# Residual linears run by thirds of the tokens in one chain, and a cross attention that writes w_xo's split inputs itself

## What is computed

```python
for layer in range(DEPTH):
    h = rms_norm(x, norm_mix_g[layer])
    y = ab_mixer(h) if layer % 2 == 0 else c_mixer(h)     # each ends in @ w_out
    x = x + y
    x = x + mem_xattn(rms_norm(x, norm_xa_g[layer]), mem_k[layer], mem_v[layer], xa_wq[layer], xa_wo[layer])
return rms_norm(x, norm_final_g)

def mem_xattn(h, mk, mv, wq, wo):          # 4 heads of 256, 256 memory tokens
    q = (h @ wq).reshape(...)
    p = softmax(einsum(q, mk) * 256 ** -0.5)
    o = einsum(p, mv)
    return o @ wo
```

## Time and profile before

| | us |
|---|---|
| median of 3 runs | 3328.08 (3316.22 to 3329.48) |
| the profiled execution, its own time | 3325.3 |
| its span, first to last instruction | 3323.6 |
| PE busy | 2883.9 (87%) |
| DVE / ACT / POOL busy | 1528.6 / 862.4 / 596.9 |
| mean granted PE clock | 0.920 of full speed |

### The profile page before, as it was taken

One profiled execution on the slowest core, in us unless ns is written; L12 is line 12 of the kernel. 1 busy time (PEld: TensorE's weight loads), 2 busy tenths in 40 slices (PEclk: granted clock), 3 DMA queues, 4 the chain that ended last, 5 costly groups with the idle time before them and its releaser, 6 DMA issues. The chain is left out here.

```text
span 3323.6 us, 46167 instructions
## 1 busy us (share of the span) xinstructions
PE 2883.9 (87%) x17599; PEld 2553.3 (77%) x17599; DVE 1528.6 (46%) x1933; ACT 862.4 (26%) x1330; POOL 596.9 (18%) x536
## 2 busy tenths in 40 slices
PE   7989999678767888888888999999898899888887
PEld 7988888334437887887578999999777789888657
DVE  6267876875466763341434121111455542340423
ACT  5211112556751011221222000011222232220231
POOL 0002222656612321200010120000322302100011
PEclk9989999889978988898998999999987899989988
DMA  7379997875134102313631322222555352213641
GB/s 263 123 246 326 366 328 259 252 218 154 33 144 141 38 32 72 104 58 133 228 111 49 114 108 83 100 95 83 182 180 189 120 178 93 99 37 122 212 153 64
DMA packets 240146, 489.51 MB, mean 147 GB/s; under 512 B 37897, under 2 KB 98954, under 8 KB 239634
## 3 DMA queue, kind: packets, MB, share of 16 engines
q1 hardware_dynamic: 220690, 420.65, 37.3%
q0 software_dynamic: 15120, 51.46, 4.4%
q10 hardware_dynamic: 4176, 15.32, 1.1%
HBM read 378.83 MB, written 112.78 MB: 148 GB/s over the span
## 5 line engine op out<-in xcount | busy, mean ns | idle before, releaser
L414 PE MATMUL ps<-in_hi,w_hi 128*128 128x344 f32 x2496 | 806.7, 323 | 93.4 <-DVE in_lo L317 93.4
L415 PE MATMUL ps<-in_lo,w_hi 128*128 128x344 f32 x2496 | 804.1, 322 | 0.0
L416 PE MATMUL ps<-in_hi,w_lo 128*128 128x344 f32 x2496 | 803.1, 322 | 0.0
L414 PEld LDWEIGHTS ps<-in_hi,w_hi 128*128 128x128 f32 x2496 | 474.7, 190 | 97.2 <-DVE in_lo L317 97.2
L416 PEld LDWEIGHTS ps<-in_hi,w_lo 128*128 128x128 f32 x2496 | 475.0, 190 | 0.0
L415 PEld LDWEIGHTS ps<-in_lo,w_hi 128*128 128x128 f32 x2496 | 474.8, 190 | 0.0
L273 DVE CAST w_hi<-w_raw 128x1024 fp32r<-128x1024 f32 x64 | 46.9, 732 | 512.9 <-PE ps L416 499.7
L277 POOL TENSOR_TENSOR w_lo<-w_raw,w_hi 128x1024 fp32r<-128x1024 f32 x40 | 95.3, 2387 | 1029.3 <-ACT w_hi L273 1029.3
L1523 PE MATMUL ps<-in_hi,wv_hi 128*128 128x344 f32 x696 | 228.4, 328 | 2.1 <-DVE wv_lo L1371 2.1
L1525 PE MATMUL ps<-in_hi,wv_lo 128*128 128x344 f32 x696 | 223.4, 321 | 0.0
L1524 PE MATMUL ps<-in_lo,wv_hi 128*128 128x344 f32 x696 | 223.4, 321 | 0.0
(11 more groups left out here) (351 smaller groups left out, 5272.7 us busy)
## 6 DMA issues: line engine op xcount, KB each, us to landing
k_pages<-in_cache_k SPq DMA_DIRECT2D x256, 256.0 KB, 4.6
v_pages<-in_cache_v POOLq DMA_DIRECT2D x160, 256.0 KB, 5.4
cc<-stage SPq DMA_DIRECT2D x48, 516.0 KB, 2.7
v_pages<-in_cache_v SPq DMA_DIRECT2D x96, 256.0 KB, 3.0
w_raw<-in_w_c SPq DMA_DIRECT2D x48, 512.0 KB, 4.3
in_raw<-og SPq DMA_DIRECT2D x40, 516.0 KB, 5.5
kq_raw<-in_w_mem SPq DMA_DIRECT2D x32, 512.0 KB, 4.0
xs_kv<-in_mem_k SPq DMA_DIRECT2D x16, 1024.0 KB, 7.2
```

What stands on the lines that cost most here:

```text
L414: pe.matmul(o, w_hi[:, u, a:b], h, start=(kt == 0), stop=False)
L415: pe.matmul(o, w_hi[:, u, a:b], l, start=False, stop=False)
L416: return pe.matmul(o, w_lo[:, u, a:b], h, start=False, stop=(kt == KT - 1))
```

## The change

`final_norm` goes, and the linears with a residual no longer use `linear`. A new function `chain` runs one to three passes as one block, all of it by thirds of the tokens: product n is output tile n % 8 of third n // 8 % 3 of pass n // 24, 24 matmuls of 344 columns, in PSUM bank n % 6. All eight weight tiles of a pass are kept, split, in SBUF (one copy; each is replaced when its last third is done), with two raw buffers. Residual additions, squares, their sums (bank 6 or 7), the scaling and the split of a normed input are each 344 columns wide and stand in each engine's order at steps n written out by `sum_at`, `norm_at`, `weight_at` and `load_at`. There is no hardware loop. The chains are w_oab + w_xq; w_xo; w_oc first half + second half + w_xq; w_xo + final norm (its last scalings, two per step, are stored in pairs of tiles). w_c keeps `linear`.

`cross_attend` gets w_xo's input buffers `hi` and `lo`. ACT's `copy_out` writes `hi` rounded, DVE's new `out_low` writes the remainder from PSUM and raises `oc_done`; nothing is stored to or loaded from `og`. The first two raw tiles of w_xo are loaded at the end of SP's queue in the attention (`early`).

The diff, cut to its core:

```diff
+def chain(k, passes, hi, lo, final=None, early=None):
...
+    BANKS, SUM_BANK = 6, 6
+    RAW = 2
+    PASS = NCH * KT
+    N = PASS * len(passes)
+    READY = passes[0].load is None
+    R = sum(p.norm is None for p in passes)
+    RES = PASS * R
+    SQ0 = RES - PASS
+    RATE = 2 if final else 1
+    END = N + (KT if final else 3)
...
+        def sum_at(n):
+            c = (n - SQ0) // KT - 1
+            return c if NORMED and 0 <= c < NCH and (n - SQ0) % KT == (3 if n < N else 2) else None
+        def norm_at(n):
+            found = []
+            for c in range(NCH):
+                first = SQ0 + KT * (c + 1) + (4 if SQ0 + KT * (c + 1) < N else 3)
+                if NORMED and first <= n < first + KT // RATE:
+                    found += [(c, RATE * (n - first) + j) for j in range(RATE)]
+            return found
+        def weight_at(n):
+            found = [m for m in (n + 2,) if 2 <= m < KT]
+            for p in range(1, len(passes)):
+                t = n - 1 - (PASS * p - KT)
+                if 0 <= t < KT:
+                    found.append(KT * p + t)
+            return found
...
+        @block.sync
...
+            def weights(m):
+                if m >= RAW:
+                    sp.wait_ge(*low(m - RAW))
+                p = passes[m // KT]
+                sp.dma_start(raw[:, m % RAW, :], p.w[p.w0 + m % KT]).then_inc(loaded[m % RAW], 16)
...
+            for n in range(END):
+                at = load_at(n)
+                if at:
+                    inputs(*at)
+                for m in weight_at(n):
+                    weights(m)
+                if RES < n <= N:
+                    store(n - 1)
...
         @block.scalar
...
+            def high(m):
+                act.wait_ge(loaded[m % RAW], 16 * (m // RAW + 1))
+                if m >= KT:
+                    act.wait_ge(mm_done, PASS * (m // KT) - KT + m % KT + 1)
+                act.copy(w_hi[:, m % KT, :], raw[:, m % RAW, :]).then_inc(hi_done, 1)
...
+            for n in range(END):
+                if sum_at(n) is not None:
+                    inverse_root(sum_at(n))
+                if RES < n <= N:
+                    evacuate(n - 1)
+                at = load_at(n)
+                if at:
+                    input_high(*at)
+                for m in weight_at(n):
+                    high(m)
+                if SQ0 < n <= RES:
+                    square(n - 1)
+                if not final:
+                    for c, kt in norm_at(n):
+                        normed_high(c, kt)
+        @block.gpsimd
+        def _(pool):
+            for m in range(int(READY), KT * len(passes)):
+                split_low(pool, m).then_inc(lo_done, 1)
+        @block.vector
...
+            for n in range(END):
+                if 0 < n <= RES:
+                    resid(n - 1)
+                if SQ0 < n - 1 <= RES and (n - 2) % KT:
+                    add_squares(n - 2)
+                at = load_at(n)
+                if at:
+                    input_low(*at)
+                if not final:
+                    for c, kt in norm_at(n - 1):
+                        normed_low(c, kt)
+                for c, kt in norm_at(n):
+                    scaled(c, kt)
...
         @block.tensor
...
+            for n in range(2, END):
+                if sum_at(n) is not None:
+                    squares_sum(sum_at(n))
...
+                if n >= BANKS:
+                    pe.wait_ge(*((resid_done, n - BANKS + 1) if n - BANKS < RES else (out_done, n - BANKS - RES + 1)))
+                for kt in range(KT):
+                    product(n, kt)
...
-def cross_attend(k, xq, kv, kv0, mem_k, mem_v, s0, og):
+def cross_attend(k, xq, kv, kv0, mem_k, mem_v, s0, hi, lo, early):
...
+            raw, loaded, w, w0 = early
             for u in range(2):
-                sp.wait_ge(stored[u], 16 * (NBATCH // 2))
+                sp.dma_start(raw[:, u, :], w[w0 + u]).then_inc(loaded[u], 16)
...
+            def out_low(n):
+                dve.wait_ge(oh_done, n + 1)
+                dve.tensor_tensor(half_of(lo, n), ps[:, 4:6, :], half_of(hi, n).bitcast(f32), ALU.subtract).then_inc(oc_done, 1)
...
             for n in range(NBATCH):
+                if n >= 1:
+                    out_low(n - 1)
                 if n + 1 < NBATCH:
                     maxima(n + 1)
                 beside(n, 0)
...
             def copy_out(n):
                 act.wait_ge(o_done, n + 1)
-                if n >= 2:
-                    act.wait_ge(stored[n % 2], 16 * (n // 2))
-                act.copy(o[:, n % 2], ps[:, 4:6, :]).then_inc(oc_done, 1)
+                act.copy(half_of(hi, n), ps[:, 4:6, :]).then_inc(oh_done, 1)
...
-        project_out(ins["w_oab"], 0, 0)
+        project_out(Pass(ins["w_oab"], 0, load=(og, 0)), queries(0))
         cross_attention(0)
...
-        for half in range(2):
-            project_out(ins["w_oc"], KT * half, KT * half, sumsq=(half == 1))
-        cross_attention(1)
-        final_norm(k, gains, G_FINAL, outs["y_t"])
+        project_out(Pass(ins["w_oc"], 0, load=(og, 0)), Pass(ins["w_oc"], KT, load=(og, KT)), queries(1))
+        cross_attention(1, final=(gains, G_FINAL, outs["y_t"]))
```

More of the change, by code:

```diff
@@ L449, in _ @@
             seq(pe, n_tiles, body)
-def final_norm(k, g, g_col, out):
-    k.recycle()
-    nc, ALU, f32, ps = k.nc, k.ALU, k.f32, k.ps
-    SLOTS = 4
-    with ExitStack() as ctx:
[L458 to L464, removed]
-        block = ctx.enter_context(nc.Block())
+@dataclass
@@ L472, in _ @@
         @block.tensor
         def _(pe):
[L474 to L493, removed]
+            def squares_sum(c):
+                pe.wait_ge(add_done, (KT - 1) * (c + 1))
+                if c >= 2:
+                    pe.wait_ge(log_done, c - 1)
+                pe.matmul(ps[:, SUM_BANK + c % 2, 0:CH], k.c("ones"), k.sumsq[:, cols(c)], start=True,
+                          stop=True).then_inc(sum_done, 1)
@@ new lines, in product @@
+            def product(n, kt):
+                t, c, a, b = n % KT, chunk_of(n), kt * 128, kt * 128 + 128
+                h, l = hi[:, kt, cols(c)], lo[:, kt, cols(c)]
+                pe.matmul(acc(n), w_hi[:, t, a:b], h, start=(kt == 0), stop=False)
+                pe.matmul(acc(n), w_hi[:, t, a:b], l, start=False, stop=False)
+                last = pe.matmul(acc(n), w_lo[:, t, a:b], h, start=False, stop=(kt == KT - 1))
+                if kt == KT - 1:
+                    last.then_inc(mm_done, 1)
@@ L2678, in _ @@
             act.wait_ge(col_done, 1)
-            act.copy(so[:, :, :].rearrange("p f s -> p (f s)"), ps[:, 7, 0:KT * S]).then_inc(so_done, 1)
+            act.copy(hi[:, :, T:NT], ps[:, 7, 0:KT * S].rearrange("p (f s) -> p f s", f=KT)).then_inc(so_done, 1)
 def rotary_tiles(k, ctx):
@@ L3113, in trunk_program, with project_out, queries, cross_attention @@
             return
-        def project_out(w, w0, tile0, sumsq=True):
+        def project_out(*passes, final=None):
             a, b = halves(NT)
             with a as hi, b as lo:
-                linear(k, w, w0, KT, hi, lo, load=(og, tile0), resid=x, sumsq=sumsq)
-        def cross_attention(layer):
+                chain(k, passes, hi, lo, final)
+        def queries(layer):
+            return Pass(ins["w_xq"], KT * layer, norm=(gains, G_XA + KT * layer), out=xq)
+        def cross_attention(layer, final=None):
             a, b = halves(NT)
-            with a as hi, b as lo:
-                linear(k, ins["w_xq"], KT * layer, KT, hi, lo, norm=(gains, G_XA + KT * layer), funcs=((KT, AF.Copy),),
-                       out=xq)
-            cross_attend(k, xq, outs["mem_kv_t"], 16 * layer, ins["mem_k"], ins["mem_v"], S * layer, og)
-            project_out(ins["w_xo"], KT * layer, 0)
-        project_out(ins["w_oab"], 0, 0)
+            with a as hi, b as lo, nc.sbuf_tensor(name("w_early"), [128, 2, KT * 128], f32) as raw:
+                loaded = [nc.alloc_semaphore(name(f"w_early{u}")) for u in range(2)]
+                cross_attend(k, xq, outs["mem_kv_t"], 16 * layer, ins["mem_k"], ins["mem_v"], S * layer, hi, lo,
+                             (raw, loaded, ins["w_xo"], KT * layer))
+                chain(k, [Pass(ins["w_xo"], KT * layer)], hi, lo, final, (raw, loaded))
+        project_out(Pass(ins["w_oab"], 0, load=(og, 0)), queries(0))
         cross_attention(0)
```

196 lines of the change are left out of this document (178 added, 18 removed).

## The result

The changed kernel takes **3277.82 us** (median of 4 runs, 3272.92 to 3281.23). The kernel before took 3327.42 beside it (4 runs, 3316.22 to 3329.48). The ratio is 0.9857, 95% interval 0.983 to 0.9883. The forecast was 3266.9, so the sign and the range were right and the gain was 11 us short of it.

A forecast was written before the change was run, and what follows sets the result against it. TensorE, busy 2883.9 of 3323.6 us, was taken as the bound, so only idle or lower-clock time could be won. Terms 49.1 + 3.0 + 0.8 + 15.4 + 18.9 - 26 = 61.2 us gave 3266.9 from the 3328.1 median; range 3244 to 3298.

The forecast's parts named there:

- Joints inside a chain: Between w_oab and w_xq and between w_oc's passes and w_xq: idle time, sums and start losses shrink, gaining 49.1 us.
- Starts: Before w_oab and w_oc, the chains that load: input loads become thirds, gaining 1.5 us each, 3.0 together.
- TensorE still waits for two remainders of 2.39: At the starts of w_oab and w_oc: GpSimd's two weight remainders still hold TensorE, so only 1.5 us each is gained.
- Ahead of the attentions: Before each cross attention: shorter evacuation and a barrier more or fewer, gaining 0.8 us in all, between -1 and 2.
- Tails: Behind the two w_xo: third-wide last operations gain 3.3 us at the first and 12.1 at the last, together 15.4.
- From attention to w_xo: Idle of 13.85 and 15.46 us before w_xo falls to about 5.2 each, gaining 18.9 us.
- The attention: In cross attention: VectorE's added subtraction delays TensorE, costing 13 us per layer, -26 us for two layers.
- The clock term: In cross attention: each of two new 4.3 us waits costs a further 2.5 us through TensorE's lower clock.
- rival 1: Cross attention's added wait is mostly hidden, 5 us per layer or less: about 3251 us; chance 0.13.
- rival 2: Weight supply falls behind in the first third of a pass nothing precedes: about 3296 us; chance 0.18 with rival 3.
- rival 3: Joined normalisation is late at passes' borders, TensorE stalls 7 us at two of three: 3281 us; chance 0.18 with rival 2.
- rival 4: TensorE sits at the lower clock in cross attention; slower beyond 31 us more full-speed work per layer there; chance 0.04.

The follow-up runs named there:

- The run with the other order: Changed kernel, but in the chains of w_oab and w_oc product 0 runs whole before product 1, second weight tile fetched after the eight input tiles: 3270.54 us.
- The table run: Changed kernel, but in chains behind the cross attention ScalarE's table load stands after the high parts of the first two weight tiles: 3271.49 us.
- the low part early: Changed kernel, but VectorE subtracts a batch's output remainder ahead of that batch's second dot products: 3248.62 us, and 3242.23 us when run again.

## Why the prediction was right, and where it was short

The sum forecast -61.2 us; the profiled executions show -45.0. By its steps:

- **Joints inside a chain**, 49.1 forecast. The two chains are 44.6 us shorter (15.46 + 29.16), although their starts lose 5.8 us more than before (next point), so the joints themselves gave 50.4. Products are 3.77 us apart, and the sums cost 0.6 us each, as forecast. Right.
- **Starts**, 3.0 forecast, -1.7 measured. The waits fell by 3.1 and 1.0. But from the first matmul to the 49th it is 12.70 and 12.76 us, where the linears of before took 9.97 and 9.67: 5.8 us more. This is the step "TensorE still waits for two remainders of 2.39": it counted the wait ahead of the first matmul only, not the second wait, 2.14 and 2.86 us, behind the first three matmuls, nor the matmuls at the lower clock around it. The run with the other order took 3.0 and 3.2 us of it away (9.71 and 9.54), which is all that the starts had lost against the kernel before.
- **Ahead of the attentions**, 0.8 forecast, 1.2 measured (-0.9 and 2.1). Right.
- **Tails**, 15.4 forecast. The joint behind the first w_xo fell from 16.24 to 13.22, and the end from 24.88 us behind the last matmul to 12.23: 15.7. Right. The last steps, VectorE's timeline:

```profile
3269.97 2.04 DVE L708 SCALAR_TENSOR_TENSOR scaled<-residual,gains_sb,rstd 128x344 f32<-128x344 f32 x4 [2.04 <-ACT rstd L636]
3273.60 2.04 DVE L708 SCALAR_TENSOR_TENSOR scaled<-residual,gains_sb,rstd 128x344 f32<-128x344 f32 x4 [1.59 <-DMA out_y_t<-scaled]
```

  The eight scalings of 0.51 and the wait of 1.59 for a stored pair are the 0.5 and 1.5 of the forecast.
- **From attention to w_xo**, 18.9 forecast. The waits fell by 20.4 and w_xo's own length rose by 1.5: 18.9. The table run confirmed the table load as a link of the chain named in the forecast; the others (block's end, rounding, remainder) stand in the same order in the timelines of ScalarE and VectorE: table load to 1680.60, rounding from 1680.61, VectorE's w_lo of 1.23 us from 1681.69, TensorE at 1682.97.
- **The attention**, -26 forecast, -29.8 measured. The waits of 4.3 us at the second and third head are 4.11, the one at the fourth is 0.52 for 0.6. The clock term, 2.5 per wait or 5 per layer, was too small: in the first attention busy time grew by 5.6 us (111.75 for 106.14) and idle time by 8.5, in the second busy time by 6.4 (112.69 for 106.27). The first one's opening was also 2.7 us quicker than in the kernel before (32 score matmuls in 5.12 and 5.41 us for 6.56 and 6.65), for no reason that these runs show, so the lower clock cost it 8.3. The forecast did not see that the outputs of the batch ahead of each of those waits would wait 2.20 for 1.73, nor that such a batch can take 5.40 us. It then took 13 where its own sum was 14.1, and 14.1 and 15.7 were measured.
- **Outside the change**, 0 forecast, -9.7 measured: 3.6 ahead of w_oab and 6.0 from the unchanged linears to the retention stage's end. This is the largest part of what was missing against the profile. No term of the sum failed here: the forecast subtracts from one execution's stages, and these stages vary from execution to execution. The stretch ahead of w_oab is 1326.58 and 1329.96 us in two executions of the kernel before. The retention stage has lasted 378.9 and 382.3 us in two executions of the kernel before, and 374.2 to 389.2 in eight of kernels that leave it alone; one kernel alone spans 374.2 to 389.0. That the changed kernel repeats at 382.6 shows that most of the +7.0 was that execution's. By the medians the gain was 49.6 us in the comparison of the result and 52.5 in the next, 9 to 12 us short of the forecast; the two terms above that were off, the starts by 4.7 and the attention by 3.8, make 8.5 of it.

So the range was met by the mechanisms that were forecast. Some luck is in the first attention: it grew by just the 14.1 us of the forecast's sum, since the lower clock took 8.3 us for 5 and the quick opening gave 2.7 back.

The rivals. A hidden wait (rival 1) did not come: both waits stand in the trace with 4.11 us. The supply of weights (rival 2) and late joints (rival 3) did not come either: TensorE has no idle time between 1346.09 and 1530.69, nor in the chain of w_oc behind 2746.99. The lower clock in the attention (rival 4) came with 6 to 8 us of busy time a layer for the 31 at which it would have decided. The rule of the Trainium skill (SBUF — State Buffer, Who interferes with whom), weighed in the forecast at up to 10 us, agrees with the traces on VectorE's side: a low part takes up to 2714 ns for 508 and ends just behind the w_lo beside it. On GpSimd's side little shows: a w_lo has a median of 2404 ns and at most 2766. The overlap cost nothing at the pace of the products, and at the starts TensorE waited for a w_lo of the usual length.

What stays open: whether the change has any effect of its own on the retention stage. Two executions of before average 380.6 us, eight of the others 384.6, and the scatter within one kernel is 15, so these numbers don't decide it. That GpSimd's w_lo holds VectorE's low parts up, and doesn't merely coincide with them, is supported by where they end but was not tried with the two kept apart. Why an attention's opening is quick in one execution and slow in the next is not shown either.

## What to carry to other kernels

When an engine takes on a new instruction that frees a buffer, its length is the small part of the price: ask what it is queued behind, and what that waits for. Here 1.22 us stood behind dot products that waited for rows of TensorE itself, and moving it one place ahead took the attentions from 29.8 us longer than before back to the lengths of before, at no cost in work. A joint between matmul stages is worth cutting into thirds whenever the normalisation of one third can lie beside the products of the next; what then decides is the start, where no lead has been built: give the first product all its inputs before the second one's weights ask for the same engines.

## What was not expected of the hardware

- A wait can cost more than itself, and a like one nothing. In the four kernels that keep this attention's order (the changed one twice, the other start, the later table load) the 16 score matmuls behind a wait of 4.11 us took 4.9 to 6.2 us in all 16 cases, for 3.62 without it. The eight outputs behind a wait of 2.20 us took 5.4 us in 10 of 16 cases and 3.70 in the other six. The length of the wait doesn't tell these apart, but what went before does: the outputs ahead of the third head, which come after a first wait of 4.11, were slow in 8 of 8, those ahead of the second head in 2 of 8, and these two are the ones in attentions with the quick opening. Behind 1.73, or 1.61 with the low part early, they took 3.70 in every batch of these traces.
- VectorE's instructions with both inputs in SBUF take longer where GpSimd's w_lo run, those that read PSUM don't. By groups of line and shape inside w_oab and w_xq (us in total, mean ns | idle before):

```profile
L708 DVE SCALAR_TENSOR_TENSOR scaled<-residual,gains_sb,rstd 128x344 f32<-128x344 f32 x24 | 22.2, 926 | 0.0
L684 DVE TENSOR_TENSOR in_lo<-in_raw,in_hi 128x344 fp32r<-128x344 f32 x24 | 22.0, 939 | 10.2 <-ACT in_hi L618 10.2
...
L690 DVE TENSOR_TENSOR residual<-ps,residual 128x344 f32<-128x344 f32 x24 | 12.3, 514 | 36.6 <-PE ps L749 36.6
```

  The scalings take 926 ns in the mean here and 510 at the end of the kernel, where no w_lo runs (four in 2.04 us). VectorE has the room: TensorE has no idle time in this stretch behind 1346.09.
- One kernel's retention stage, unchanged, took 389.0 and 374.2 us in two executions, two thirds of it busy time of equal matmuls at another clock. A difference of 10 us in this stage of one profile is no evidence here; a difference of 3 us in the chains, which repeat to 0.9 and 1.3 us over the six executions with the same chains, is, and so is one of 1.28 in the waits for w_xo, which repeat to 0.01.
